# Softmax attention with the query block outermost and token-major values, and a token-innermost expert multiply

## What is computed

```
def diff_attention(q, k, v, lam, lam_init, subln_g):
    ...
        sc = jnp.where(causal, sc, -jnp.inf)
        p = jax.nn.softmax(sc, axis=-1)
        a = p[:, :, 0] - lam * p[:, :, 1]
        return jnp.einsum('bhqs,bshd->bqhd', a.astype(v.dtype), v)
    ...
    o = rms_norm(o, subln_g) * (1.0 - lam_init)
def chunk(args):                     # experts: 128 of 16384 a token
    a = jnp.einsum('cd,ced->ce', hc, u[ic])
    a = jax.nn.gelu(a, approximate=False) * gc.astype(hc.dtype)
    return jnp.einsum('ce,ced->cd', a, v[ic])
```

## Time and profile before

| | |
|---|---|
| time, median of 3 runs | 2422.77 us (2417.9 to 2424.58) |
| profiled execution, its own time | 2421.13 us |
| its span | 2419.3 us |
| PE, DVE, ACT busy | 2053.6 (85%), 1635.0 (68%), 1225.6 (51%) us |
| PE clock granted, mean of the span | 0.887 |

### The profile page before, as it was taken

How to read it: one execution, slowest core, us unless ns; L and a number is a source line. 1 busy time by engine, 2 the same in 40 slices (tenths; PEclk the granted TensorE clock), 3 DMA queues, 4 the chain that set the end, 5 groups by cost and what they waited for, 6 DMA issues and landing times. The chain is left out here.

```text
span 2419.3 us, 44273 instructions
## 1 busy us (share of the span) xinstructions
PE 2053.6 (85%) x15728; PEld 1935.8 (80%) x15728; DVE 1635.0 (68%) x3333; ACT 1225.6 (51%) x2388; POOL 31.4 (1%) x39
## 2 busy tenths in 40 slices
PE   7964887999999866899999784796998966989896
PEld 6942685999999855899999774696898955689895
DVE  5667656599945599766666557865677567658855
ACT  4433344577765698455555454102565533355643
POOL 0020000000000000000000000000000002000000
PEclk9975688899999978999999896786999988589998
DMA  5610242355555400355555340001464422035451
GB/s 204 195 50 0 70 140 72 121 174 174 175 198 192 155 0 0 130 192 191 193 194 193 114 139 18 1 1 50 157 199 161 145 87 96 1 123 195 159 173 61
DMA packets 95217, 295.98 MB, mean 122 GB/s; under 512 B 9203, under 2 KB 25718, under 8 KB 94582
## 3 DMA queue, kind: packets, MB, share of 16 engines
q1 hardware_dynamic: 95094, 294.35, 36.3%
HBM read 293.26 MB, written 1.05 MB: 122 GB/s over the span
## 5 line engine op out<-in xcount | busy, mean ns | idle before, releaser
L300 DVE TENSOR_TENSOR w_low<-ring,w_high 128x512 fp32r<-128x512 f32 x1102 | 747.8, 690 | 467.2 <-ACT w_high L294 463.8
L326 PE MATMUL bank<-a_high,w_high 128*128 128x256 f32 x3256 | 931.1, 286 | 130.5 <-DVE a_low L575 68.4
L294 ACT ACTIVATE w_high<-ring 128x512 fp32r<-128x512 f32 x1102 | 680.7, 628 | 492.0 <-PE bank L328 488.6
L327 PE MATMUL bank<-a_low,w_high 128*128 128x256 f32 x3256 | 921.0, 283 | 0.0
L328 PE MATMUL bank<-a_high,w_low 128*128 128x256 f32 x3256 | 920.1, 283 | 0.0
L326 PEld LDWEIGHTS bank<-a_high,w_high 128*128 128x128 f32 x3256 | 630.6, 194 | 142.6 <-issue 103.9
L327 PEld LDWEIGHTS bank<-a_low,w_high 128*128 128x128 f32 x3256 | 631.0, 194 | 0.3
L328 PEld LDWEIGHTS bank<-a_high,w_low 128*128 128x128 f32 x3256 | 629.0, 193 | 0.0
L326 PE MATMUL bank<-s_high,w_high 128*128 128x256 f32 x1024 | 284.0, 277 | 2.7 <-DVE s_low L1631 2.7
L327 PE MATMUL bank<-s_low,w_high 128*128 128x256 f32 x1024 | 283.7, 277 | 0.0
L328 PE MATMUL bank<-s_high,w_low 128*128 128x256 f32 x1024 | 283.7, 277 | 0.0
(11 more groups left out here) (294 smaller groups left out, 2149.4 us busy)
## 6 DMA issues: line engine op xcount, KB each, us to landing
ring<-in_stream SPq DMA_DIRECT2D x279, 512.0 KB, 4.0
ring<-in_peer_u SPq DMA_DIRECT2D x128, 512.0 KB, 3.5
ring<-in_peer_v SPq DMA_DIRECT2D x128, 512.0 KB, 3.4
ring<-in_stream SPq DMA_DIRECT2D x32, 256.0 KB, 3.2
consts<-in_consts SPq DMA_DIRECT2D x1, 1024.0 KB
x<-in_x SPq DMA_DIRECT2D x1, 1024.0 KB, 7.0
arena<-in_mem SPq DMA_DIRECT2D x1, 1024.0 KB, 9.0
out<-x SPq DMA_DIRECT2D x1, 1024.0 KB, 3.9
```

The lines of the kernel that those rows point to most:

```text
L294: self.nc.scalar.activation(self.w_high[:, h % SLOTS, :], self.raw(h), ACT.Copy)\
L300: self.nc.vector.tensor_tensor(self.w_low[:, h % SLOTS, :], self.raw(h), self.w_high[:, h % SLOTS, :].bitcast(F32), ALU.subtract)\
L326: self.nc.tensor.matmul(to, lh, rh, start=start, stop=False, **more)
L327: self.nc.tensor.matmul(to, lh, rl, start=False, stop=False, **more)
```

## The change

Four things, in `attention` unless said otherwise.

- The units ("steps", one a score map) come in groups: all of query block 0, then all of block 1. Every step now has its own exponential, its own transposes and its own product with the values, two maps of a head too.
- Factor, mask and maximum become one `tensor_tensor_reduce` (the build makes two DVE instructions of it, marked ISA), with the sign turned, and the exponential has scale -1. Where there is no mask, or only in part, a mask of 256 columns is filled once.
- The probabilities are not divided. They are the weights of L860 and the values move, so the result has tokens on partitions: 64 or 128 columns a step, eight or four steps in a bank. A group is divided by its sums in one multiply of 128 x 512 (`norm`), turned by four transposes (`face`) and copied out (`take`). The differential attention has two multiplies and a subtract instead and is left token-major.
- `norm_heads` works token-major: squares and sums on DVE, reciprocal and root on 128 x 8, eight transposes, and a multiply out of PSUM. In `expert_weights` the merge has the four tokens innermost.

```diff
+                def turn(f):
+                    keys = flat[f][2]
+                    pe.wait_ge(expd.sem, expd.at(f + 1))
...
+                def mix(f):
+                    _, _, keys, _, _, values, bank, col = flat[f]
+                    pe.wait_ge(held.sem, held.at(f + 1))
+                    if f in starts and starts.index(f) >= apart:
+                        pe.wait_ge(normed.sem, normed.at(starts.index(f) - apart + 1))
...
-                        ins = nc.tensor.matmul(self.bank[6 + u % 2][units[u][3]:units[u][3] + dv, 0:P], values[j],
-                                               pt[u % 2][:, j * P:(j + 1) * P], start=j == 0,
-                                               stop=j == keys // P - 1)
+                        ins = nc.tensor.matmul(self.bank[bank][:, col:col + dv],
+                                               pt[f % 2][:, j * P:(j + 1) * P], values[j],
+                                               start=j == 0, stop=j == keys // P - 1)
...
+                for i in steps:
+                    if i < n:
+                        score(i)
+                    if 0 <= i - 2 < n:
+                        turn(i - 2)
+                    if 0 <= i - 4 < n:
+                        mix(i - 4)
+                    if i - 5 in ends and lam is None:
+                        face(ends.index(i - 5))
...
+                    nc.vector.tensor_tensor_reduce(
+                        out=sc[f % 4][:, 0:keys], in0=self.bank[f % 3][:, 0:keys], in1=more,
+                        scale=-factor, scalar=3e38, op0=ALU.add, op1=ALU.min,
+                        accum_out=least[:, f:f + 1]).then_inc(scaled.up(), 1)
...
+                    link(nc.vector.tensor_scalar(pairs[:, :, 1], pairs[:, :, 1], lam, None, ALU.mult))
+                    nc.vector.tensor_tensor(split(kept[g]), split(self.bank[5][:, :]),
+                                            over(pairs[:, :, 0]), ALU.mult)
+                    link(nc.vector.tensor_tensor(split(kept[2]), split(self.bank[6][:, :]),
+                                                 over(pairs[:, :, 1]), ALU.mult))
+                    link(nc.vector.tensor_tensor(kept[g], kept[g], kept[2], ALU.subtract))
...
+                link(nc.vector.tensor_tensor(squares, heads, heads, ALU.mult))
+                link(nc.vector.tensor_reduce(size, squares, AX, ALU.add))
+                link(nc.vector.tensor_scalar(size, size, 1.0 / P, EPS, ALU.mult, ALU.add))
+                nc.vector.reciprocal(size, size).then_inc(mean.up(), 1)
...
-                    part = scores[:, bass.ds(it * each + b * batch, batch), :]
+                    part = scores[:, :, bass.ds(it * each + b * batch, batch)]
                     nc.vector.tensor_tensor(part, part, self.bank[b % step][:, :].rearrange(
-                        "p (t j) -> p t j", t=batch), ALU.mult).then_inc(merged.sem, 1)
+                        "p (t j) -> p j t", t=batch), ALU.mult).then_inc(merged.sem, 1)
```

More of the change, by code:

```diff
@@ L811, in _, with attention @@
                         .then_inc(along.up(), 1)
-    def attention(self, units, work):
+    def attention(self, groups, work, kept, fill=None, lam=None):
         nc = self.nc
[L820 to L824, removed]
+        scored, scaled, expd, turned, held, mixed, normed, faced, done, filled = (
+            self.counter(s) for s in ("scored", "scaled", "expd", "probs_turned", "probs_kept",
+                                     "mixed_values", "heads_normed", "heads_turned",
+                                     "attention_out", "mask_filled"))
+        flat = [unit for units, _ in groups for unit in units]
+        ends = [sum(len(units) for units, _ in groups[:g + 1]) for g in range(len(groups))]
+        starts = [0] + ends[:-1]
+        n = len(flat)
         sc = [work[:, i, :] for i in range(4)]
         pt = [work[:, 4 + i, :] for i in range(2)]
+        mask = work[:, 6, :]
         stat = self.small[:, 256:512]
+        least, sums, parts = stat[:, 0:64], stat[:, 64:128], stat[:, 128:192]
+        apart = 1 if lam is not None else 2
+        steps = range(n + 7)
         with nc.Block(no_gpsimd_drain=True) as block:
@@ L831, in score @@
                 def score(f):
[L832 to L839, removed]
@@ L863, in mix, with face @@
                     ins.then_inc(mixed.up(), 1)
[L865 to L873, removed]
+                def face(g):
+                    pe.wait_ge(normed.sem, normed.at(g + 1))
+                    if g:
+                        pe.wait_ge(done.sem, done.at(g))
+                    for c in range(4):
+                        ins = nc.tensor.transpose(self.bank[7][:, c * P:(c + 1) * P],
+                                                  kept[g % 2][:, c * P:(c + 1) * P],
+                                                  self.const("ident"))
+                    ins.then_inc(faced.up(), 1)
@@ L879, in scale @@
                 def scale(f):
-                    u, m = flat[f]
-                    _, keys, factor, mask, _ = units[u][0][m]
+                    _, _, keys, factor, more, _, _, _ = flat[f]
                     dve.wait_ge(scored.sem, scored.at(f + 1))
                     if f >= 4:
[L884 to L897, removed]
@@ L898, in scale @@
-                    link(ins)
[L899 to L937, removed]
+                        dve.wait_ge(turned.sem, turned.at(f - 3))
@@ new lines, in take @@
+                def take(g):
+                    dve.wait_ge(faced.sem, faced.at(g + 1))
+                    nc.vector.tensor_copy(groups[g][1],
+                                          self.bank[7][:, :].rearrange("p (c t) -> p c t", c=4))\
+                        .then_inc(done.up(), 1)
+                if fill is not None:
+                    ins = nc.vector.memset(mask, 0.0)
+                    if fill == "causal":
+                        link(ins)
+                        ins = nc.vector.tensor_copy(mask[:, P:T], self.const("causal_add"))
+                    link(ins)
@@ L939, in _ @@
+                for i in steps:
+                    if i < n:
+                        scale(i)
+                    if i - apart - 2 in ends:
+                        norm(ends.index(i - apart - 2))
+                    if i - 6 in ends and lam is None:
+                        take(ends.index(i - 6))
             @block.scalar
             def _(act):
[L941 to L949, removed]
@@ L1180, in memory @@
                       after=(self.fetched, 16))
-        units = [([([(q[:, h, b * P:(b + 1) * P], kmem[:, h, :])], T, P ** -0.5, None, None)],
-                  [vm[:, j, h * P:(h + 1) * P] for j in range(2)], out[:, h, b * P:(b + 1) * P], 0)
-                 for h in range(4) for b in range(TT)]
-        self.attention(units, work)
+        flat = self.at(32 * T, 2, 512)
+        groups = [([(q[:, h, b * P:(b + 1) * P], kmem[:, h, :], T, P ** -0.5, work[:, 6, :],
+                     [vm[:, j, h * P:(h + 1) * P] for j in range(2)], 5 + b, h * P)
+                    for h in range(4)], out[:, :, b * P:(b + 1) * P]) for b in range(TT)]
+        self.attention(groups, work, [flat[:, i, :] for i in range(2)], "none")
         self.products([("mem_o", "fm", out, None)])
@@ L1470, in expert_weights @@
                                      "merged"))
[L1471 removed]
+        scores = self.arena[:, 0:N_KEYS * T].rearrange("p (j t) -> p j t", t=T)
         iota = self.const("iota")
```

178 lines of the change are left out of this document (99 added, 79 removed).

## The result

The changed kernel takes 2361.09 us (2355.14 to 2365.22 over 4 runs) against 2421.69 beside it; the ratio is 0.974 (0.971 to 0.977). That is some 60 us, and the forecast was 2414, with a range that ended at 2388. The profiled execution is 2359.31, its span 2357.5.

The account below looks back on a forecast made before the run. Limits were taken stage by stage: a chain in the differential attention and `norm_heads`, PE in the other attentions, DVE in the experts. -16.0 + 8.9 - 8.6 + 3.4 + 5.5 + 1.8 - 2.0 = -7.0 from 2421.13 gave 2414, range 2388 to 2435.

Parts of the forecast that it names:

- -8.6: `norm_heads`: with the smaller reciprocal and the new token-major steps it takes 7.1 us against 15.7.
- The experts' mechanism: Experts' weights: the merge gets faster, DVE stops being the limit, 1.98 us a batch; -16.0, at most -19.8.
- the low bound: Experts' merge: 687 ns instead of 1285, if SBUF runs of four tokens suffice and PSUM steps cost nothing.
- The first rival: Experts' merge stays slow because of strided PSUM reads; experts give nothing, whole kernel at 2430 us; chance 0.24.
- PE's work a pair stays: Sparse, memory and MLA attention: PE's time per pair is unchanged (4.56 us in sparse).
- the turnings: New PE transposes per group, 1.06 us, with a 2.3 tail: sparse +3.4 (one and tail), MLA +5.5 (three and tail).
- the -2.0: Sparse and MLA: products with 64 instead of 128 columns moving save half of a possible 4.3 us.
- the clock rises: 128-column weights and 256-key steps standing together bring PE's full clock; 22 us, whole kernel at 2392 us; chance 0.19.
- DVE's saving is off the path: Sparse, memory and MLA attention: PE is the limit, so what DVE saves there is worth nothing.
- +8.9: Differential attention: twice the transposes and products make PE the limit, 41.3 us against 32.4.
- PE's wait for the first division: Differential attention: PE stands about 1.0 us, with hand-offs, while the first group is divided.
- a loss of 1.8: Memory attention: PE's stage, so new transposes and the tail add 1.8 us, with a mask to fill first.

Follow-up runs that it names:

- the alternating blocks: Changed kernel with 128-key and 256-key steps alternating in the sparse and latent attention, as before the change; 2360.62 us, MLA 36.2 us.
- the merge alone: Kernel before with only the token-innermost merge in the experts' weights; 2402.53 us, ratio 0.990.

## Why the prediction was wrong

**What held.** `norm_heads` (-8.5 against -8.6). The experts' mechanism: the merge at the low bound, and ACT as the next limit, busy 114.94 of 125.40. The term's size was off: I charged 44% of the batches at PE's low-clock pace, from the old window's 0.78, but the clock there is 0.90 now, and the gain is the -19.8 that the working had as its bound. The first rival falls with it. Advanced Engine Details and Errata of the Trainium skill (Memory Cachelines) wants every two consecutive elements contiguous in PSUM, next to a sentence on matmuls. A DVE read in steps of 128 floats at 686 ns against 687 does not agree with that, if it is meant for DVE's reads too.

**The step that failed: "PE's work a pair stays".** In sparse and MLA I left PE's time for a pair as it was (4.56 us in the earlier trace rows), as the price of the operations. It was the price of these operations next to each other. In the earlier trace rows each unit goes from a 64-row score to a 128 x 128 transpose to a product with 64 columns of weights, and such neighbours cost PE time: at one clock, 1.56 us a step with 64 columns against 1.07 in MLA, and 1.44 with 64 rows against 1.06 with 128 in sparse. In sparse, at 0.50 before and after, the pair went from 4.56 to 3.96 us (1.44, and 2.52 from 243.35 to 245.87), which outweighs the turnings and gives the -3.1; 0.1 a step of it is the narrower moving operand (1.55 and 2.62 in the run with 128 columns moving). TensorEngine Tiling (Array Packing) of the Trainium skill (Key Properties) says that a change of the tiling mode, not of the tile alone, drains TensorE. These steps agree, though no trace shows the mode, and the page gives no price. Making the probabilities the weights removed the column changes in sparse and MLA, and the diff shows it in one line. I read that line for the moving width only, and in MLA, where most of the -2.0 was to come from, that gave nothing: a step takes 1.07 us with 64 columns moving and with 128. There the pair of 4.34 us became 1.07 and 2.13 at the same clock; that is, as an estimate, 16 x 1.14 or some 18 of its 32.2 us.

**The rival that came in one stage.** I gave "the clock rises" 0.19 and 22 us, and named the right mark, products with 128 columns of weights; its sign, a clock above 0.6 in the 256-key halves, came in MLA, from 2040 on, while sparse stayed at 0.50. As an estimate it is worth some 16 us there: 16 steps of 256 keys at 1.11 instead of 2.13. It was given 22 for three stages. The change beat this rival's 2392 by 31 us, mostly because the pairs became shorter at the low clock too. I had tied the clock to the 256-key steps standing together, which the alternating blocks refute. What brought it sooner in these runs was fuller rows, fuller columns, wider moving operands and alternating blocks; what delayed it was the product nearer to its transposes. PE was 93 to 96% busy at 0.50 in the earlier trace rows, so its busy share told nothing of it.

**What was not on the list.** MLA was held by three limits, one behind the other. In the kernel before, full columns take it from 71.0 to 57.3, the division left out to 54.5, and the product a unit later to 39.2, which is nearly the whole change (in another order the shares differ: a unit later with the division kept gives 5.2). I wrote that DVE's saving is off the path there and did not look at the order on PE at all: product four steps behind its score, two behind its transposes, stands in the diff. Undone singly in the changed kernel, columns cost 19.3 us, the distance 9.8 (by the clock, not by a wait), the fused instruction 3.2; they overlap, so that they come to 32.3 is chance.

**Smaller terms.** The differential cost +3.3 and not +8.9. Its steps are 1.56 and 2.62 us at the low clock, not 1.74 and 2.82, with no change of columns among them (165.37 to 166.93 and 183.36 to 185.98 in PE's timeline); that is some 3 of the 5.6 us. What is left over by subtraction lies at the stage's two ends, the last 4.6 us of it at a clock of 0.99. PE's wait for the first division was 0.95, as forecast. Memory gained 1.9 where I had a loss of 1.8. I had called it PE's, and the merge alone shows that it was not: there, with the old attention and the clock at 1.00, it takes 14.5 us from its first to its last instruction, against 14.7 at 0.88 before and 12.8 after. With the product sooner it is 14.3 at 1.00, so the distance mattered. The fused instruction undone costs 1.9, but about 1.0 of that can be the clock: two runs that leave this stage alone take 13.8 and 13.9 us in it at 0.88.

**What stays open.** The shares of MLA's gain, some 18 us at the same clock and some 16 by the clock (turnings and ends take about 2 back), are estimates from steps, and the 2.13 is from a kernel with another order on PE. Whether the low clock comes from the empty rows and columns or from the stops at each change was not tried, nor why the order on PE moves it.

## What to carry to other kernels

A price read from a timeline belongs to an operation and its neighbours: before keeping it, see whether the change alters the shape that stands beside it. Fill all rows and columns of a weight tile, with zeros or with a neighbour's values whose product is thrown away, wherever small tiles alternate with 128 x 128 ones; it cost at most a few us of copies here and gave 11 to 15 us in three stages, where the clock rose with it. In the sparse stage full columns beside 64-row scores gave 2.1, with the clock at 0.50 throughout. And when a stage is said to be PE's at the low clock, ask what would hold it at the high one, since that limit comes next.

## What was not expected of the hardware

Multiplying more could cost nothing, or even save time: 128 columns moving instead of 64 left a step of MLA at 1.07 us, and scores with 64 rows of zeros added made sparse 19.8 us instead of 35.0. A fused multiply, add and minimum over 128 x 256 from PSUM took 424 ns, no more than a plain pass over as much, and 83 ns more for its accumulator. A DVE read of PSUM in steps of 128 floats cost nothing against a contiguous one (686 ns against 687).
